# One pipeline over all 32 attention items instead of two passes over 16, with q scaled at the projection

## The reference, cut to what matters

```python
def diff_attention(q, k, v, rel_bias, lam, subln_g, lam_init):
    scale = DIFF_HEAD_DIM ** -0.5
    def block(args):
        q_blk, i = args
        ...
        logits = jnp.einsum('bqhcd,bkhcd->bhcqk', q_blk, k).astype(jnp.float32) * scale
        logits = logits + bias.transpose(2, 0, 1)[None, :, None]
        logits = jnp.where((dist >= 0)[None, None, None], logits, -jnp.inf)
        p = jax.nn.softmax(logits, axis=-1)
        attn = p[:, :, 0] - lam * p[:, :, 1]
        return jnp.einsum('bhqk,bkhe->bqhe', attn.astype(v.dtype), v)
    ...
    out = rms_norm(out, subln_g) * (1.0 - lam_init)
```

## Time and profile before

| | |
|---|---|
| median of three runs | 2837.85 us |
| the profiled execution | 2833.64 us |
| its span | 2831.9 us |
| TensorE / VectorE / ScalarE busy over the span | 94% / 82% / 45% |
| the attention, from its first logits to its last output | 320.3 to 480.0 us of the span |
| granted TensorE clock over the span | 0.975 (1.0 is 2.4 GHz, 0.5 is 1.2 GHz) |

### The profile page before, as it was taken

How to read it: one execution, slowest core, us unless ns; L and a number is a source line. 1 busy time by engine, 2 the same in 40 slices (tenths; PEclk the granted TensorE clock), 3 DMA queues, 4 the chain that set the end, 5 groups by cost and what they waited for, 6 DMA issues and landing times.

```text
span 2831.9 us, 42694 instructions
## 1 busy us (share of the span) xinstructions
PE 2658.2 (94%) x15119; PEld 2346.1 (83%) x15119; DVE 2322.1 (82%) x4258; ACT 1267.3 (45%) x2434; POOL 1095.5 (39%) x779
## 2 busy tenths in 40 slices
PE   7999776879998999999999999997999999999998
PEld 4888544768888999999999999996888887888886
DVE  3462477456989999999899876668999999999998
ACT  4111466232122298989999892222222222222222
POOL 0000000001113344444444755544666766666662
PEclk9999888989999999999999999998999999999999
DMA  6640000314347789999999999999999999999997
GB/s 237 236 169 13 10 0 15 119 60 135 127 143 251 274 289 318 325 310 326 294 323 319 389 404 394 376 339 335 403 406 399 399 406 401 396 406 401 402 405 264
DMA packets 326101, 794.38 MB, mean 281 GB/s; under 512 B 28832, under 2 KB 127808, under 8 KB 324416
## 3 DMA queue, kind: packets, MB, share of 16 engines
q0 software_dynamic: 110592, 402.70, 38.0%
q1 hardware_dynamic: 195776, 343.68, 34.2%
q10 hardware_dynamic: 19584, 46.15, 4.1%
HBM read 694.11 MB, written 98.30 MB: 280 GB/s over the span
## 4 chain that ended last, share of the span: by engine, by line
PE 45%; DVE 16%; DMA 9%; issue 6%; ACT 1%; SPq 0%; DVEq 0%; ACTq 0%
PE ps_up L418 35%; DVE row_sum L120 9%; DMA stage<-v_cols 7%; PE ps_g L465 5%; PE ps_y L829 4%; DMA stage<-expert_act 2%; DVE coef_lo L904 1%; DVE acc L883 1%; ACT v_hi L796 1%; PE ps_g L433 1%; DVE fetched L115 1%; DVE topi L525 0%; DVE col_lo L510 0%; SPq L756 0%; DVE top L522 0%
## 5 line engine op out<-in xcount | busy, mean ns | idle before, releaser
L97 POOL DMA_INDIRECT fetched<-u_rows,row_index x384 | 550.1, 1433 | 701.6 <-DVE row_act L115 585.4
L97 POOL DMA_INDIRECT fetched<-v_cols,row_index x384 | 541.2, 1409 | 356.0 <-DVE row_sum L120 298.2
L418 PE MATMUL ps_up<-h_hi,col_hi 128*128 128x320 f32 (+1 forms) x2288 | 553.3, 322 | 30.6 <-DVE col_lo L510 14.1
L418 PE MATMUL ps_up<-h_lo,col_hi 128*128 128x320 f32 (+1 forms) x2288 | 545.6, 318 | 0.0
L418 PE MATMUL ps_up<-h_hi,col_lo 128*128 128x320 f32 (+1 forms) x2288 | 545.3, 318 | 0.0
L120 DVE SCALAR_TENSOR_TENSOR row_sum<-fetched,row_act,row_sum 128x1024 f32<-128x1024 f32 x381 | 487.2, 1279 | 1.5 <-DVE row_sum L120 0.5
L115 DVE CUSTOM_DVE_ANT_0 fetched<-fetched,h_rows_then_gates 128x1024 f32<-128x1024 f32 x384 | 451.7, 1222 | 18.2 <-DMA fetched<-u_rows,row_index 7.6
L829 PE MATMUL ps_y<-v_hi,coef_hi 128*128 128x512 f32 x1280 | 398.4, 393 | 34.6 <-DVE coef_lo L904 31.5
L418 PEld LDWEIGHTS ps_up<-h_hi,col_hi 128*128 128x128 f32 x2288 | 385.6, 189 | 42.5 <-issue 32.4
L796 ACT ACTIVATE v_hi<-stage 128x1024 fp32r<-128x1024 f32 x128 | 136.0, 1062 | 636.2 <-DMA stage<-v_cols 629.7
L418 PEld LDWEIGHTS ps_up<-h_hi,col_lo 128*128 128x128 f32 x2288 | 388.9, 189 | 10.8
(11 more groups left out here) (247 smaller groups left out, 3479.7 us busy)
## 6 DMA issues: line engine op xcount, KB each, us to landing
stage<-cols SPq DMA_DIRECT2D x144, 512.0 KB, 6.9
stage<-v_cols SPq DMA_DIRECT2D x128, 512.0 KB, 8.3
expert_act<-stage ACTq DMA_DIRECT2D x128, 320.0 KB, 6.2
stage<-expert_act SPq DMA_DIRECT2D x128, 320.0 KB, 6.3
z_t<-w_ada SPq DMA_DIRECT2D x48, 512.0 KB, 6.0
expert_gate<-g_buf SPq DMA_DIRECT2D x40, 512.0 KB, 11.3
g_raw<-expert_gate SPq DMA_DIRECT2D x64, 320.0 KB
h_rows_then_gates<-expert_gate SPq DMA_DIRECT2D x64, 320.0 KB, 9.8
```

Of the source, the lines that this page charges most:

```text
L97: nc.gpsimd.indirect_dma_start(self.buf[:, n % NBUF], None, rows, bass.IndirectOffsetOnAxis(ap=self.at[:, tile, k:k + 1], axis=0)).then_in ...
L418: mm = pe.matmul(ps_up[:, b, half, 0:width], w[:, b, k], h[:, k, a:a + width], start=(k == 0 and i == 0), stop=(k == DC - 1 and i == 2))
```

## The change

The loop of two passes is gone. One list `ITEMS` has all 32 items, tile by tile with four heads in each: tiles 1, 3, 5, 7, 6, 4, 2, 0, four items of each. All 32 are written out, with constant addresses. The eviction of q at L1285 carries the scale 1/8, so that the scaling of q, the copy of k and the copy of the bias values go, and the logits read `z_t` in place. On ScalarE `far_part` now stands ahead of `exps`, and `squares` comes two items later instead of one. VectorE's and TensorE's steps keep their order. The name of the change also speaks of gates stored by group from two blocks: that code stands in both kernels alike, and the diff doesn't touch it.

```diff
@@ -1282,7 +1282,8 @@
-                        nc.scalar.activation(z_t[:, m], ps[:, j], ACT.Gelu_apprx_tanh if p < 2 else ACT.Copy).then_inc(copied, 1)
+                        nc.scalar.activation(z_t[:, m], ps[:, j], ACT.Gelu_apprx_tanh if p < 2 else ACT.Copy,
+                                             scale=DH ** -0.5 if p in (4, 5) else 1.0).then_inc(copied, 1)
...
-        pair_qk = z_t[:, 0:4]
+        q, k = z_t[:, HEADS_A:2 * HEADS_A], z_t[:, 2 * HEADS_A:3 * HEADS_A]
...
-        PAIR = 2 * TT
-
         rising = list(range(1, TT, 2))
-        ORDER = [(a, i) for i in rising + [i - 1 for i in rising[::-1]] for a in range(2)]
-        FAR = [0]
-        for m in range(PAIR):
-            FAR.append(FAR[-1] + (ORDER[m][1] >= 2))
+        ITEMS = [(h, i) for i in rising + [i - 1 for i in rising[::-1]] for h in range(HEADS_A)]
+        N = len(ITEMS)
+        FAR = [sum(i >= 2 for _, i in ITEMS[:g]) for g in range(N + 1)]
...
         @block.scalar
...
-            with loop(nc, act, 0, HEADS_A // 2) as w:
-                act.wait_ge(pair_free, w + 1)
-                nc.scalar.activation(pair_qk[:, 2:4], z_t[:, bass.ds(8 + 2 * w, 2)], ACT.Copy).then_inc(pair_ready, 1)
-                far_part(w, 0)
-                far_part(w, 1)
-                exps(w, 0)
-                for m in range(PAIR):
-                    if m + 1 < PAIR:
-                        exps(w, m + 1)
-                    if m + 2 < PAIR:
-                        far_part(w, m + 2)
-                    copy_t(w, m)
-                    if m >= 1:
-                        squares(w, m - 1)
-                squares(w, PAIR - 1)
-                act.wait_ge(sq_sum, PAIR * w + PAIR)
+            far_part(0)
+            far_part(1)
+            exps(0)
+            for g in range(N):
+                if g + 2 < N:
+                    far_part(g + 2)
+                if g + 1 < N:
+                    exps(g + 1)
+                copy_t(g)
+                if g >= 2:
+                    squares(g - 2)
+            squares(N - 2)
+            squares(N - 1)
+            act.wait_ge(sq_sum, N)
...
         @block.tensor
...
-            with loop(nc, pe, 0, HEADS_A // 2) as w:
-                pe.wait_ge(pair_free, w + 1)
-                logits(w, 0)
-                logits(w, 1)
-                for m in range(PAIR):
-                    if m + 2 < PAIR:
-                        logits(w, m + 2)
-                    if m >= 1:
-                        values(w, m - 1)
-                    turn(w, m)
-                values(w, PAIR - 1)
+            logits(0)
+            logits(1)
+            for g in range(N):
+                if g + 2 < N:
+                    logits(g + 2)
+                if g >= 1:
+                    values(g - 1)
+                turn(g)
+            values(N - 1)
...
         @block.vector
...
-            ch.reset()
-
-            dve.sem_inc(pair_free, 1)
-            with loop(nc, dve, 0, HEADS_A // 2) as w:
-
-                nc.vector.tensor_scalar(pair_qk[:, 0:2], z_t[:, bass.ds(4 + 2 * w, 2)], DH ** -0.5, None, ALU.mult).then_inc(pair_ready, 1)
-                nc.vector.tensor_copy(far_pair[:], far[:, bass.ds(2 * w, 2)]).then_inc(pair_ready, 1)
-                for m in range(2):
-                    near(w, m)
-                    maximum(w, m)
-                for m in range(PAIR):
-                    combine(w, m)
-                    if m + 2 < PAIR:
-                        near(w, m + 2)
-                        maximum(w, m + 2)
-                    if m >= 1:
-                        output(w, m - 1)
-                output(w, PAIR - 1)
-                dve.wait_ge(o_done, PAIR * w + PAIR)
-                dve.sem_inc(pair_free, 1)
-                ch.reset()
+            for g in range(2):
+                near(g)
+                maximum(g)
+            for g in range(N):
+                combine(g)
+                if g + 2 < N:
+                    near(g + 2)
+                    maximum(g + 2)
+                if g >= 1:
+                    output(g - 1)
+            output(N - 1)
```

More of the change, by code:

```diff
@@ L1601, in far_part @@
[L1601 to L1605, removed]
-                for c in range(2):
[L1607 to L1615, removed]
-                nc.scalar.activation(att_t[:, m % 2, 0:n], ps_t[:, 0:n], ACT.Copy).then_inc(t_copied, 1)
@@ new lines, in far_part @@
+                if g >= NL:
+                    act.wait_ge(comb_done, g - NL + 1)
+                bias = far[:, h:h + 1]
+                copy = nc.scalar.activation(logit[:, g % NL, :, 0:min(n, HALF)], ps_first[:, :, 0:min(n, HALF)], ACT.Identity, bias=bias)
+                if n > HALF:
+                    act.wait_ge(near_done, g + 1)
+                    copy = nc.scalar.activation(logit[:, g % NL, :, HALF:n], ps_rest[:, :, 0:n - HALF], ACT.Identity, bias=bias)
+                copy.then_inc(far_done, 1)
@@ new lines, in exps, with copy_t @@
+            def exps(g):
+                n = (ITEMS[g][1] + 1) * P
+                act.wait_ge(max_done, g + 1)
+                for c in range(2):
+                    nc.scalar.activation(logit[:, g % NL, c, 0:n], logit[:, g % NL, c, 0:n], ACT.Exp, bias=nmax[:, g % 2, c:c + 1],
+                                         accum_out=ssum[:, g % 2, c:c + 1]).then_inc(exp_done, 1)
+            def copy_t(g):
+                n = ITEMS[g][1] + 1
+                act.wait_ge(t_done, g + 1)
+                if g >= 2:
+                    act.wait_ge(o_mm, g - 1)
+                nc.scalar.activation(att_t[:, g % 2, 0:n], ps_t[:, 0:n], ACT.Copy).then_inc(t_copied, 1)
@@ L1686, in values @@
+            def values(g):
+                h, i = ITEMS[g]
+                pe.wait_ge(t_copied, g + 1)
+                if g >= 2:
+                    pe.wait_ge(o_done, g - 1)
+                col = SW + h * VD
                 for j in range(i + 1):
-                    mm = pe.matmul(ps_o[:, m % 2, 0:VD], att_t[:, m % 2, j], z_n[:, j, bass.ds(col, VD)],
-                                   start=(j == 0), stop=(j == i))
+                    mm = pe.matmul(ps_o[:, g % 2, 0:VD], att_t[:, g % 2, j], z_n[:, j, col:col + VD], start=(j == 0), stop=(j == i))
@@ L1727, in _, with near @@
             ch.sync()
[L1729 to L1731 removed]
+            def near(g):
+                h, i = ITEMS[g]
                 k0, width = (i - 1) * P if i else 0, 2 * P if i else P
[L1733 to L1737 removed]
@@ L1739, in maximum @@
-            def maximum(w, m):
-                g = PAIR * w + m
-                n = (ORDER[m][1] + 1) * P
+                dve.wait_ge(l_done, 2 * g + 2)
+                if g >= NL:
+                    dve.wait_ge(comb_done, g - NL + 1)
+                bias = tb[:, h:h + 1, 2 * P - width:2 * P].to_broadcast([P, 2, width])
+                at = max(0, k0 - HALF)
+                nc.vector.tensor_tensor(logit[:, g % NL, :, k0:k0 + width], ps_rest[:, :, at:at + width], bias, ALU.add).then_inc(near_done, 1)
```

115 lines of the change are left out of this document (46 added, 69 removed).

## The result

The changed kernel took 2798.81 us (median of 4 runs, 2797.48 to 2799.96) beside 2837.51 us (4 runs, 2833.62 to 2838.15) for the kernel before: ratio 0.9861, 95% interval 0.9849 to 0.9873. The forecast was 2807.4 with a range of 2801 to 2817. The sign and the order of size were right; the gain is 8 us larger than predicted.

A forecast was written before the change was run, and what follows sets the result against it. In the attention no engine was full: VectorE and ScalarE took turns waiting, with further loss at the passes' edges. Terms -6.7 - 3.65 - 0.4 - 21.6 + 2.0 = -30.4 us took 2837.85 to 2807.4 us, range 2801 to 2817.

The forecast's parts named there:

- Part 1, the seam: Between the attention's two passes: making them one removes the seam and waits for first logits, minus 6.7 us.
- the 0.4 of the first items: First pass of the attention: 0.4 us of its 0.95 us of waits for first logits goes.
- Part 2, the start: Attention's start: without copies the first near bias can start about 0.1 us behind `neg_lam`, minus 3.65 us.
- Part 3, the order: ScalarE's order in each attention item: VectorE's maxima lose 4.7 us waiting for far parts instead of 26.3, minus 21.6 us.
- The tie at tiles 6 and 7: Second far part needs the same item's near bias and precedes its maximum: eight waits of 0.5 to 0.7 us, 4.7 us stay.
- register instructions that go (0.05 us each, under other work) I count at nothing: Looped passes of the attention: dropping the loop's register instructions was taken to gain nothing.
- Part 4, the clock: TensorE in the attention: low clock at the start costs plus 2.0 us, bounds 0 and 5; low stretches mid-stage become rarer.
- everything behind it has its length of before: Stages after the attention: they wait for its last output at a barrier and keep their lengths, so its gain is the kernel's.
- a change of a later stage's length as a sign of being wrong: Stages after the attention: the prediction is wrong if a later stage changes its length.
- the four rivals: Whole kernel: waits persist, 2829 us, 10%; TensorE bounds, 2819 us, 5%; slower, 2878 us, 2%; same time, 1%.
- The wait under another name: ScalarE's in-order copy holds back the next far part, VectorE's 26.3 us stay: gain 8.8 us, 2829 us; chance 10%.
- TensorE as the bound: Attention: at a low-clock share of 0.4 TensorE needs 141 us and decides: gain 19 us, 2819 us; chance 5%.

The follow-up runs named there:

- experiment 6: Kernel before with ScalarE's new order and the two passes written out, copies and seam kept: 2809.16 us, ratio 0.9891, attention stage 161.6 us.
- experiment 7: Changed kernel with the copies of q and k put back at its start: 2802.62 us, ratio 0.9866, attention stage 155.2 us.
- experiment 3: Kernel before with only ScalarE's new order: 2822.46 us, ratio 0.9932, attention stage 166.4 us.
- experiment 2: Changed kernel with ScalarE's old order put back: 2815.85 us, ratio 0.9914, attention stage 172.5 us.
- experiment 5: Kernel before with only its two passes written out instead of looped: 2825.44 us, ratio 0.9953, attention stage 180.9 us.
- Experiment 4: Changed kernel with one order edit undone: exponentials ahead of far part again, 2806.14 us; or squares one item back again, 2799.44 us.
- experiment 1: Both kernels run again: the kernel before, ratio 0.9995; the changed kernel, 2797.33 us, ratio 0.984.
- experiment 9: Changed kernel plus 12 float32 matmuls of 128 x 256 in TensorE's idle start: 2793.06 us; control with 12 tiny ones: 2795.62 us.
- experiment 8: Small float32 matmuls padded ahead of the attention's first logits: 38 in the kernel before, 2837.41 us; 26 in the changed kernel, 2804.71 us.

## Why the prediction was right in kind and too small

| term | forecast | measured in the attention stage |
|---|---|---|
| seam and first items | -6.7 and -0.4 | -5.9 (experiments 6 and 7) |
| start | -3.65 | -3.5 (experiments 6 and 7) |
| ScalarE's order | -21.6 | -18.9 to -20.2 (experiments 3 and 2), -19.3 from experiment 5 to 6 |
| written out instead of looped | 0 | -4.4 (experiment 5) |
| TensorE's clock | +2.0 | no difference seen |
| stage | -30.4 | -33.0 |
| behind the stage | 0 | -5 to -9 |

- **Part 1, the seam,** with the 0.4 of the first items was 1.2 us too dear.
- **Part 2, the start,** was right in mechanism and size: the near bias follows `neg_lam` directly, 3.5 for 3.65.
- **Part 3, the order:** size nearly right, reason only half right. The tie at tiles 6 and 7 is there eight times as said, 6.1 us in place of 4.7, the longest 1.2 where 0.7 was expected. But I wrote that ScalarE "no longer stands for VectorE" because the squares go two items back. Experiment 4 shows that the place of the far part does all of it: what counts is not that ScalarE waits, but what is queued behind the wait. Far part first, the wait holds only work that nobody needs soon.
- **Written out:** "register instructions that go (0.05 us each, under other work) I count at nothing". The 0.05 us lies on VectorE, ahead of 26 outputs. This is 1.4 of the 4.4 us and the seam's turn 0.7; 0.5 us lie at the two ends, and 1.8 us within the passes were not traced. The term is larger than the stage's whole error of 2.6. I looked for what straight code costs (new code, 0.25 us) and not for what it saves. That the stage came within 2.6 us is partly luck: the seam and the order were 3.5 us too large, the loop and the clock 6.4 too small.
- **Part 4, the clock:** at the 13 to 17 us of low clock that the changed kernel's profiles have, no run shows the 2.0 us. Whether 10 or 17 us between near bias 0 and the last output ran at the low level, that stretch took 128.8 to 129.1 us (experiments 1, 7 and 9). Only in the padded changed kernel (experiment 8), with 25 us at the low level, did it become 130.2. That the low stretches in the middle would get rarer was right: the profile of the result has none from 332 to 444 us.
- **The step that failed** is "everything behind it has its length of before", from which I took that "what the stage gains the kernel gains". I argued it from data alone: nothing was prefetched by time. TensorE's own instructions are fetched too (queue 8), and the change made the queue ahead of a rolled loop longer. That, by experiment 8, takes the stops at the loop's turns away, which is worth about 13 us of routing (1284.3 us in the mean of the four profiles with them, 1271.4 in that of the five without any stop); the new stop at 817 us takes a part of this back, and 5 to 9 us are left. With the 33.0 us of the stage alone the same sum would have come to 2804.9 us, inside the range. The prediction named a change of a later stage's length as a sign of being wrong, but gave it neither a price nor a chance.
- **The range:** its low end of 2801 rested on the stage's terms only and had no room for a change elsewhere, nor for the 4.2 us between the profile and the median, carried over as exact.

None of the four rivals took place. The wait under another name: 6.1 us left, not 26.3. TensorE as the bound: 0.4 us of VectorE waiting for logits.

## What to carry to other kernels

Where two engines take turns, ask of each wait what is queued behind it and who wants that: put the work that the other engine needs next ahead of the wait, and the wait itself may stay. When a change makes an engine's straight code longer or shorter, every rolled loop behind it on that engine moves too; compare the idle time marked "issue" at the loop's turns in stages that the change does not touch, and pad before you believe a small gain or loss. Whether the code is being fetched at such a stop can be seen on the DMA queue marked "instruction". And compare stage by stage with a second profile of each kernel, since the stages here scatter by up to 4 us by themselves.

## What was not expected of the hardware

- A turn of TensorE's rolled loop cost 2.3 to 3.7 us of standing still and, in nine of twelve cases, a short stretch at the lower clock, together 4.1 to 4.9 us for a pass, or no stop at all, with the same loop body and only the number of instructions ahead of it changed. The Trainium skill, "Runtime: NRT & Kernel Launch", section "Instruction fetch mechanics", says that instructions are fetched in order in blocks of 16 KiB (256 instructions) and that a taken branch outside of the fetched window stalls. The packets of queue 8, 16 KiB each, and the stops in before agree; but the changed kernel takes the same three branches without a stop, so here the rule is not enough to tell the cost. The number of blocks in a pass, ten or nine, went with it in all 18 profiles.
- The same section calls the crossing of a block in straight code mostly hidden. Here one stop of 2.6 to 5.6 us in straight code appeared in six of seven profiles with the changed kernel's TensorE code, and TensorE went on 2.3 to 2.5 us behind the start of a packet of queue 8.
- VectorE's output starts 0.05 us later behind `nmax` in the rolled loop, where its address is computed in a register, than in straight code.
- In the kernel before queue 8 moved no packet from 370.2 to 480.1 us, though TensorE executed the whole second pass (656 matmul and weight load records) in that time: it ran from what it already held. A pass of L480 is fetched anew each time, in nine or ten packets.
